# One stage of a decode-step kernel with other buffer counts, another order of ScalarE in its opening, and exponentials and memory stores moved to its end

## The reference

```python
h = rmsnorm(x, norm1_g)                      # prompt 2048 x 1024, samples 8 x 1024
b, c, hc, q, k, v, f, q_m = split(h @ w_in)  # w_in 1024 x (3*256 + 3*512 + 8 + 256)
logf = log_sigmoid(f + b_f)
y_conv = b * causal_conv3(c * hc)
y_fox = softmax(q k' / 8 + cumsum(logf)_q - cumsum(logf)_k, causal) v     # 8 heads of 64
mk, mv = split(rmsnorm(mem, mem_norm_g) @ w_mem_kv)                       # 256 memory tokens
y_mem = softmax(q_m mk' / 8) mv                                           # 4 heads of 64
x = x + (concat(norm(y_conv), norm(y_fox), norm(y_mem)) * out_norm_g) @ w_out
x = rmsnorm(x + (silu(h2 @ w_gate) * (h2 @ w_up)) @ w_down)               # h2 = rmsnorm(x)
```

## Time and profile before

| | |
|---|---|
| median of three runs | 2884.95 us (2879.7 to 2886.36) |
| the profiled execution | 2879.7 us, its span 2878.0 us |
| PE busy | 2702.5 us, 94% |
| PEld, DVE, POOL, ACT busy | 2433.0, 1721.4, 1607.3, 1151.1 us |
| mean granted TensorE clock | 0.981 |
| largest DMA queue (the hardware queue, loads and stores) | 451.96 MB, 54.0% of 16 engines' span |

### The profile page before, as it was taken

The page is one execution under the profiler, slowest core; times in us unless marked ns, Lnnn a source line. Parts: engine busy times, 40 slices in busy tenths (PEclk is TensorE's granted clock), DMA queues, the critical chain, the costliest instruction groups (busy, mean ns, idle before and its releaser), DMA issues. The chain is left out here.

```text
span 2878.0 us, 42283 instructions
## 1 busy us (share of the span) xinstructions
PE 2702.5 (94%) x15137; PEld 2433.0 (85%) x15137; DVE 1721.4 (60%) x2246; ACT 1151.1 (40%) x1924; POOL 1607.3 (56%) x903
## 2 busy tenths in 40 slices
PE   8999999888999888899879999999999989999998
PEld 7998989777777777677779999999999977888887
DVE  5375686477788877676475657565756553224332
ACT  4212312466666667533343334333433332113221
POOL 3476688498879989365256665666655620000111
PEclk9999999899999999999989999999999999999999
DMA  6587889667666666676443333333246437445553
GB/s 210 174 271 248 262 269 304 159 163 188 175 179 170 181 186 183 193 229 212 129 141 118 96 101 116 129 108 118 79 118 150 96 95 216 132 133 165 163 163 108
DMA packets 483758, 476.76 MB, mean 166 GB/s; under 512 B 154951, under 2 KB 380034, under 8 KB 482518
## 3 DMA queue, kind: packets, MB, share of 16 engines
q1 hardware_dynamic: 464830, 451.96, 54.0%
q10 hardware_dynamic: 18432, 21.05, 2.1%
q0 software_dynamic: 288, 1.05, 0.1%
HBM read 392.83 MB, written 81.14 MB: 165 GB/s over the span
## 5 line engine op out<-in xcount | busy, mean ns | idle before, releaser
L2377 PE MATMUL ps_gate_up<-h_hi,w_hi 128*128 128x344 f32 (+1 forms) x1848 | 593.4, 321 | 36.6 <-DVE h_lo L2298 31.1
L2379 PE MATMUL ps_gate_up<-h_hi,w_lo 128*128 128x344 f32 (+1 forms) x1848 | 593.5, 321 | 0.0
L2378 PE MATMUL ps_gate_up<-h_lo,w_hi 128*128 128x344 f32 (+1 forms) x1848 | 592.9, 321 | 0.0
L2377 PEld LDWEIGHTS ps_gate_up<-h_hi,w_hi 128*128 128x128 f32 x1848 | 349.5, 189 | 41.0 <-issue 17.4
L2378 PEld LDWEIGHTS ps_gate_up<-h_lo,w_hi 128*128 128x128 f32 x1848 | 349.7, 189 | 0.0
L2379 PEld LDWEIGHTS ps_gate_up<-h_hi,w_lo 128*128 128x128 f32 x1848 | 349.7, 189 | 0.0
L867 PE MATMUL ps_proj<-w_hi,h_hi 128*128 128x428 f32 (+1 forms) x800 | 288.7, 361 | 9.8 <-ACT proj_out L591 9.7
L2643 PE MATMUL ps_down<-wd_hi,act_hi 128*128 128x512 f32 x704 | 275.2, 391 | 13.2 <-DVE wd_lo L2565 13.2
L868 PE MATMUL ps_proj<-w_lo,h_hi 128*128 128x428 f32 (+1 forms) x800 | 285.3, 357 | 0.0
L869 PE MATMUL ps_proj<-w_hi,h_lo 128*128 128x428 f32 (+1 forms) x800 | 284.6, 356 | 0.0
L1540 DVE TENSOR_TENSOR p_lo<-ps_turned,p_hi 128x512 fp32r<-128x512 f32 (+1 forms) x352 | 214.6, 615 | 108.9 <-ACT p_hi L1447 106.7
(11 more groups left out here) (313 smaller groups left out, 6346.5 us busy)
## 6 DMA issues: line engine op xcount, KB each, us to landing
shared_pages<-in_cache_k SPq DMA_DIRECT2D x192, 256.0 KB, 3.4
common<-in_cache_v SPq DMA_DIRECT2D x172, 256.0 KB, 3.0
common<-in_w_gate SPq DMA_DIRECT2D x33, 1024.0 KB, 7.1
common<-in_w_up SPq DMA_DIRECT2D x33, 1024.0 KB, 5.9
shared_pages<-out_proj SPq DMA_DIRECT2D x48, 512.0 KB, 7.1
spare<-act_turned SPq DMA_DIRECT2D x16, 1408.0 KB, 8.1
act_raw<-act_turned SPq DMA_DIRECT2D x16, 1408.0 KB, 8.0
page_v<-in_cache_v SPq DMA_DIRECT2D x84, 256.0 KB, 3.1
```

The costliest lines, as they stand in the source:

```text
L2377: pe.matmul(acc, a_hi, h_hi[:, m, d, 0:n], start=d == 0, stop=False)
L2378: pe.matmul(acc, a_hi, h_lo[:, m, d, 0:n], start=False, stop=False)
L2379: mm = pe.matmul(acc, a_lo, h_hi[:, m, d, 0:n], start=False, stop=d == H - 1)
```

## The change

The change has five parts. KEYS goes from 4 to 3: the page buffer of its own goes, and `page_k` is `shared.pages`. SPLIT goes from 5 to 6. The zero rows get a tile of their own and are stored at step 12, not at step 3, and the wait for that store moves from the first key load to the end of the stage. In the opening ScalarE has the weight splits ahead of the turned tiles in every step. And the exponentials of the samples' scores and the stores of the memory k and v move from the first slots of attention to the end of the projection; the scores' exponential becomes one instruction in place of two, and GpSimd's two waits for them go.

```diff
-    RAWS, SPLIT, XS, OUTS, KEYS = 3, 5, 5, 4, 4
+    RAWS, SPLIT, XS, OUTS, KEYS = 3, 6, 5, 4, 3
...
-        key_pages_3 = sb("key_pages", [P, 4, FW])
-        zero = q_row[0:PAD, 0, :]
+        zero = sb("zero_rows", [PAD, 2 * CW])
...
-        page_k = [shared.pages[:, k] for k in range(3)] + [key_pages_3[:]]
+        xn, page_k = shared.rows, shared.pages
...
                     if g == 0:
...
-                        sp.wait_ge(s.zero_out, 16)
...
+                def store_memory(n):
+                    _, b, _, _, _ = step_of(n)
+                    for k, t in enumerate(tiles_at(n)):
+                        e = evacuated_by[n, k]
+                        sp.wait_ge(s.evac, e)
+                        sp.dma_start(io.mem_kv[t * P:(t + 1) * P, b * MW:(b + 1) * MW], kept[:, e - MAIN_ROWS - 1, :]).then_inc(c.kept, 16)
...
-                    if n == 3:
-                        sp.wait_ge(s.zeroed, 1)
-                        sp.dma_start(scratch.proj[0:PAD, CW:3 * CW], zero).then_inc(s.zero_out, 16)
                     if n == 12:
                         sp.dma_start(b_row[0:DB, :], io.b_f.to_broadcast([DB, FH])).then_inc(s.bias, 16)
+                        sp.wait_ge(s.zeroed, 1)
+                        sp.dma_start(scratch.proj[0:PAD, CW:3 * CW], zero[:]).then_inc(s.zero_out, 16)
...
+                    if n - 1 in groups and n - 1 >= MAIN:
+                        store_memory(n - 1)
...
-                    if n < 0:
-                        for job in jobs_at(n):
-                            turned_hi(*job)
                     for item in items_at(n, SPLIT_BEFORE):
                         split_hi(item)
-                    if n >= 0:
-                        for job in jobs_at(n):
-                            turned_hi(*job)
+                    for job in jobs_at(n):
+                        turned_hi(*job)
...
+                act.wait_ge(s.shifted, 1)
+                act.activation(dec.scores[:], dec.scores[:], ACT.Exp).then_inc(s.weighed, 1)
+                act.activation(dec.mem_scores[:], dec.mem_scores[:], ACT.Exp).then_inc(s.weighed, 1)
+                act.activation(dec.w_new[0:DB, :], small[0:DB, 4, :], ACT.Exp).then_inc(s.weighed, 1)
+                act.wait_ge(s.weighed, 3)
```

In `attend` the same things go away:

```diff
-                    if n == 2:
-                        for half in range(2):
-                            for t in range(2):
-                                sp.dma_start(io.mem_kv[t * P:(t + 1) * P, half * MW:(half + 1) * MW], a.kept[:, 2 * half + t, :]).then_inc(c.kept, 16)
...
-                    if g == 0:
-                        pool.wait_ge(s.raised, 1)
-                    if g == PGROUPS:
-                        pool.wait_ge(s.raised, 4)
...
-                    if n == 1:
-                        act.activation(dec.scores[:, 0:PAGES * FH], dec.scores[:, 0:PAGES * FH], ACT.Exp).then_inc(s.raised, 1)
-                    if n == 2:
-                        act.activation(dec.scores[:, PAGES * FH:], dec.scores[:, PAGES * FH:], ACT.Exp).then_inc(s.raised, 1)
-                        act.activation(dec.mem_scores[:], dec.mem_scores[:], ACT.Exp).then_inc(s.raised, 1)
-                        act.activation(dec.w_new[0:DB, :], dec.w_new[0:DB, :], ACT.Exp).then_inc(s.raised, 1)
```

More of the change, by code:

```diff
@@ L290, in project_all @@
         hs = sb("h_sample", [P, DT * 2 * DB + P - 2 * DB], F32R)
-        xn = shared.rows
+        xn, page_k = shared.rows, shared.pages
         junk = common[:, at:at + D]
@@ L334, in project_all @@
                  "st0 st1 st2 st3 zeroed zero_out ready s_made s_row s_fold s_out s_stored s_kept "
[L335 removed]
+                 "q0 q1 keys0 keys1 keys2 pool_done prod_done keys_done "
                  "g_turned g_z g_low g_abs g_exp g_ln g_logf g_scan g_tok_made g_off g_offset g_cum g_tok_out g_stored logf_stored gs_x gs_low gs_abs gs_exp gs_ln gs_logf gs_out "
[L337 removed]
+                 "const_filled const_shaped const_done tables same masked scanned offsets cum_made cum_turned row_major qm_in seq seq_max own_in link maxed peak_turned peak_wide all_max shifted weighed head_in")
         with stage(nc, names) as (block, s):
             x_in, w_load = (s.x0, s.x1, s.x2, s.x3, s.x4), (s.w0, s.w1, s.w2)
[L340 removed]
+            stored, q_in, keys_in = (s.st0, s.st1, s.st2, s.st3), (s.q0, s.q1), (s.keys0, s.keys1, s.keys2)
             def lo_done(item):
@@ L354, in key_product @@
                 kind, at = ENTRIES[g]
-                part = page_k[g % KEYS]
+                part = page_k[:, g % KEYS, :, :]
                 if kind == "mem":
@@ L411, in load_keys @@
                         page = sp.value_load(c.pages[0:1, 4 * at + j:4 * at + j + 1], min_val=0, max_val=last_page)
-                        sp.dma_start(page_k[g % KEYS][:, j, :], key_pages[ds(page, 1)].rearrange("n r c -> (n r) c")).then_inc(keys_in[g % KEYS], 16)
+                        sp.dma_start(page_k[:, g % KEYS, j, :], key_pages[ds(page, 1)].rearrange("n r c -> (n r) c")).then_inc(keys_in[g % KEYS], 16)
+                def store_memory(n):
[4 more added lines that the diff above has]
+                        sp.dma_start(io.mem_kv[t * P:(t + 1) * P, b * MW:(b + 1) * MW], kept[:, e - MAIN_ROWS - 1, :]).then_inc(c.kept, 16)
                 def store_sample(k):
@@ L488, in _ @@
                 sp.wait_ge(s.s_stored, 16 * NB - 16)
+                sp.wait_ge(s.zero_out, 16)
                 sp.wait_ge(s.logf_stored, 16 * (NT + 1))
@@ L520, in _ @@
                 pool.memset(hs[:].bitcast(F32), 0.0).then_inc(s.ready, 1)
-                pool.memset(zero, 0.0).then_inc(s.zeroed, 1)
+                pool.memset(zero[:], 0.0).then_inc(s.zeroed, 1)
                 pool.wait_ge(s.const_shaped, 3)
@@ L717, in keys @@
                     sums = dec.mem_scores[:, at * 4 * 2 * MH:(at + 1) * 4 * 2 * MH] if kind == "mem" else part_scores[:, at % 8 * 4 * FH:(at % 8 + 1) * 4 * FH]
-                    dve.tensor_reduce(sums, page_k[g % KEYS].rearrange("p a (h d) -> p (a h) d", d=HD), AX.X, ALU.add).then_inc(s.keys_done, 1)
+                    dve.tensor_reduce(sums, page_k[:, g % KEYS, :, :].rearrange("p a (h d) -> p (a h) d", d=HD), AX.X, ALU.add).then_inc(s.keys_done, 1)
                     if kind == "page" and at % 8 == 7:
@@ L811, in _ @@
                 link(dve.tensor_reduce(small[0:DB, 3, :], wide[0:DB].rearrange("p b h -> p h b"), AX.X, ALU.add))
-                dve.tensor_tensor(dec.w_new[0:DB, :], small[0:DB, 2, :], small[0:DB, 3, :], ALU.subtract).then_inc(s.shifted, 1)
+                dve.tensor_tensor(small[0:DB, 4, :], small[0:DB, 2, :], small[0:DB, 3, :], ALU.subtract).then_inc(s.shifted, 1)
             @block.tensor
```

13 lines of the change are left out of this document (5 added, 8 removed).

## The result

The changed kernel takes 2900.15 us (median of 6 runs, 2896.39 to 2910.03) against 2883.07 for the kernel before on the same chip: ratio 1.0065, 95% interval 1.0046 to 1.0084, thus 17.1 us by the medians and 13 to 24 by the interval. It is slower, as forecast, and 2900.15 lies inside the range 2881 to 2904, but the forecast of +7 was too small by 10 us, and 17.1 lies beyond the +2 to +12 that the forecast gave itself. The profiled execution took 2901.98 us, span 2900.3, against 2879.7 and 2878.0.

What follows compares the result with a forecast made beforehand. TensorE (PE), busy 94% of 2878.0 us, was taken to bound the kernel. Key buffers +6, split buffers 0, opening +1.5, zero rows 0 and boundary -0.5 gave +7: 2892 on the median, range 2881 to 2904.

Steps and rivals of the forecast that it cites:

- the long stall: PE's wait near 412 us for ScalarE's evacuation, 6.8 us before the change, expected at 10 to 14 us.
- rival 2: Lag spreads to block ends near 451, 489 and 370: two more stalls with clock loss, 2x5.6 = 11; 2903, chance 0.13.
- signs of being wrong: Stall near 412 at most 7 us, a new w_lo wait or second evacuation wait, or ScalarE last at the barrier.
- Opening: Before step 0: the second split delays the turned halves and PE's next transposes; +1.5, bounds 0.5 and 2.2.
- Key buffers, the walk to the long stall: Groups 43 to 45 issue later with three buffers, so a weight load and PE's stall come 4.3 us later.
- the third rival: VectorE's product of group 41 escapes GpSimd, reductions come earlier and the 6.8 us stall goes; faster, 2877, chance 0.08.
- Key buffers elsewhere: Other block ends of this half, near 451 and 489 us, with late groups in front: 1 us added.
- Split buffers: ScalarE may split one PE step earlier; PE waits for no split, so nothing, bounds 0 and -1.
- Zero rows: Same memset, store moved from step 3 to step 12 between waiting weight loads: nothing either way.
- Barrier: Stage's end: four stores taking 1.94 us make SP last and move the barrier by +1.9.
- Exponentials out of attention: First attention slots: without table load and exponentials ahead, PE's waits of 1.8 and 1.3 shrink by 2.4 in all.
- the boundary as a whole: Projection's end and first attention slots together: +1.9-2.4 = -0.5, bounds -1.2 and +2.7.

Runs made afterwards that it cites:

- k3: Three key buffers in place of four in the kernel before, the unused fourth tile staying allocated; ratio 1.0045, 13 us slower.
- after_pool_late: Changed kernel, with GpSimd's first value product waiting until VectorE's first write of v_stacked is done; ratio 1.0042 to the kernel before.
- opening: Kernel before, with ScalarE's weight split placed ahead of the turned tiles in steps before 0; ratio 1.0008, 2 us.
- exps: Kernel before, with the four exponentials of the decode weights moved from attention to the projection's end; ratio 1.0005, 1.4 us.
- after_act_stores: Changed kernel, with the four memory stores issued from ScalarE's queue in place of SyncE's; ratio 1.0047 to the kernel before.
- k3_early8: Kernel before with three key buffers and step 72's weight load two steps earlier in SP's queue; ratio 1.0034.

## Why the sum was too small, step by step

The sign, the long stall and the opening came out. That the time fell into the stated range is in part luck: the size was wrong in three terms, all in the direction of slower, and the nearest figure is not the forecast's 2892 but the 2903 of rival 2, whose two stalls of 5.6 us with their clock loss came out as waits of 1.05 and 0.76. Of the prediction's own signs of being wrong one appeared, the further evacuation waits at 372.76 and 501.03; and the barrier's gap (7.8, said: 5.5) and the wait for scores (3.3, said: near nothing) missed theirs.

- **Opening, +1.5.** Right: +1.8 in the trace. PE's second transposes start at 15.35 (said: 15.5), the wait is 3.43, and the split of 13.08 stands ahead of the two turned halves at 13.90 (said: 13.96).
- **Key buffers, the walk to the long stall, +4.3 (6.9 with delays that feed on each other).** Right. Less the shift that k3 already had there (5.4, at 369.9), its groups 43, 44 and 45 issue 7.3, 8.8 and 7.9 us later (said: 7.3, 8.7 and 6.3), the load of step 75 leaves 5.4 later (said: 4.3), and the stall grows by 5.5. (The prediction does not spell out its step from 6.3 to 4.3. The trace before gives 4.2: SP had 3.35 us between the load at 387.62 and the next key load at 390.97, and needs 1.19 where nothing holds it, as at 406.77.) The escape of a VectorE product, the third rival, took place in part: one product took 2.28 us in place of 6.19 near 398 us, and the load was late all the same.
- **Key buffers elsewhere, +1.** Wrong in size, and the largest error: outside the long stall (5.6) the buffer cost another 4.6 us in the changed kernel (1.4 near 282, 1.2 near 369, 0.9 near 489, the rest in smaller steps), and 13.3 less 5.5 is 7.8 in k3. Two of them are the second rival's spread lag, which was worked out as two stalls of 4 us; they are 1.05 and 0.76 (1.97 and 1.77 in k3). The third, near 282 us, no case contained. There the buffer did not delay a load that PE waits for: GpSimd's product comes to lie on VectorE's, and the gate work behind it comes late. All six kernels with three key buffers have it, and two of the eight with four, so not all of it can be charged to the buffer. I had used such a meeting only as an argument for a faster kernel. k3 gives the whole term as 13 us by the clock and in its trace, taking the buffer back out of the changed kernel as 12, the changed kernel's own trace as 10, with whatever the split buffers and the zero rows do in it.
- **Split buffers, 0.** No wait for a split appears. The experiment leaves -12 to +1 us open.
- **Zero rows, 0.** Nothing of it is seen; not tried by itself.
- **Barrier, +1.9.** Order right, size wrong: SP is last, ScalarE ends 2.65 us ahead of it. The move is +4.2, as four issues behind the first head's loads take 4.52 us and not 1.94. The row I priced them by had its issues at a quiet place of the queue; the row beside it, L147 with 2.40 for one issue, should have warned. The stores alone show the same (4.00), and ScalarE's queue at the same time does not (1.92).
- **Exponentials out of attention, -2.4.** Right by itself: PE's wait for k_stacked goes from 1.8 to 0.5 and the shift falls by 2.7. What was late next was missing: the write of v_stacked also comes 2.7 us earlier, into GpSimd's product. The shift rises by 2.7 at once and to 17.3 by 564.9 us, as PE is slower behind the stall (granted clock 0.68 from 573 to 582 us, where after_pool_late has 1.00 from 568 to 578; the 128x512 matmul at 573.01 takes 0.77 us, the same one in after_pool_late 0.47); undoing the meeting gives 5.9 us back. So the boundary as a whole is +5.3 (12.0 to 17.3), not -0.5.

With these sizes, 1.8 + 10.2 + 5.3 is 17.3. The Trainium skill's page SBUF — State Buffer (section "SBUF: two separate sides") says of the two engines that the later one blocks until the first has done; here that holds at the two meetings in the changed kernel shown above: the write of v_stacked ends 1.08 us behind the product that held it (571.04 and 572.12), VectorE's key product 2.16 us behind (278.75 and 280.91), each little less than its own length alone, 1.22 and 2.28.

The parts alone add up to 0.0084 and the changed kernel has 0.0065. Stores and exponentials share one barrier (gaps of 7.61 and 4.82 alone, 7.77 together, 3.60 with neither), which is 1.1 us of the difference; both also pay for a late write of v_stacked. The rest is within the intervals.

Open: at 1026.5 us the changed kernel loses up to 5.6 us, as a later write of v_stacked (1041.27, 4.48 us) meets GpSimd's product of 1041.03. The same step is in opening, exps, after_pool_late, after_act_stores and k3_early8, and in none of the other seven. In those six traces the write starts 0.1 to 0.5 us behind the product and takes 4.2 to 4.6 us; in the others, the kernel before among them, it starts 0.1 to 0.8 us ahead and takes 1.2 to 1.9, and the product takes 4.6. That a write 0.3 to 0.8 us ahead takes 1.4 to 1.9 and not its 1.22 alone is more than the page says, and its cause is open. So it goes with the phase in which a kernel reaches that slot; I have one trace of each and can't say how often either comes. It is not needed for the 17.1 us of the medians.

## What to carry to other kernels

An engine that is taken off the path releases work downstream at another moment: ask not only what becomes free, but which other engine's work the freed work now meets. Holding GpSimd's product back by 1.0 us (from 7.6 to 8.6 behind the barrier) gave 5.9 us in the trace. When a buffer ring is cut, look at the whole stage for waits of the same form as the worst one, not at the worst one alone. And price a DMA issue by the issues next to the place where it goes, not by the same issue at its old place.

## What the runs showed that I had not expected

- Four stores of 128x256 took 1.94 us to issue on SP in a quiet stretch, 4.52 and 4.00 behind the 512 KB loads of the first head in the same queue, and 1.92 from ScalarE's queue beside the last of those loads.
- When VectorE's write and GpSimd's product meet, the one that starts second is the one that is long, even if the other is ahead by less than 0.1 us: with the write 0.06 us ahead 1.23 and 4.65, with the write 0.09 us behind (exps, 1026.34 and 1026.25) 4.63 and 3.64.
- The table load of 1.28 us was begun while ScalarE's next instruction still had a wait to meet: it starts at 552.49, straight behind the last evacuation, the subtraction waited for ends at 553.65, and the exponential starts 0.01 us behind the load's end.
